# First-kind feed-forward taken on x times the norm weight, with the inverse root multiplied in afterwards

## The chip, the cores and the metric

The kernel runs on one core of one Trainium2 chip. The metric is the device time of one execution in microseconds (us). The core's engines are TensorE (PE in the profile, with its weight loads as PEld), VectorE (DVE), ScalarE (ACT), GpSimd (POOL) and SyncE (SP, which here only issues DMAs). Each engine works through its own instructions in the order in which they were written, and waits on semaphores for the others.

## What is computed

Two transformer blocks of a first kind run one after the other, then two of a second kind, on 512 tokens of width 1024 in float32. The change touches the first kind alone. One of its layers, cut to what matters here:

```python
m = hybrid_mixer(rms_norm(x, norm_mix_pre), ...)      # ends in a product with w_out
x = x + rms_norm(m, norm_mix_post)                    # norm N2
h = rms_norm(x, norm_ffn_pre)                         # norm N3
g, u = jnp.split(h @ w_gate_up, 2, axis=-1)           # 1024 -> 2 x 2816
f = (jax.nn.silu(g) * u) @ w_down
x = x + rms_norm(f, norm_ffn_post)                    # norm N4

def rms_norm(x, g): return x * lax.rsqrt(jnp.mean(x * x, -1) + eps) * g
```

Beside this the second kind needs a "modulation" for each of its layers, silu(c) @ w_mod: one vector of 48 x 128 numbers from a weight of 48 parts of 512 KB each. The first-kind layers compute it on DVE while TensorE works on the feed-forward.

## The kernel before

The state x lies transposed in SBUF as xT, 8 channel tiles (KT = 8) of 128 channels by 512 tokens. Every product is made in three passes: both operands are split into a high part and a rest (hHi and hLo for activations, wHi and wLo for weights), and each tile of 128 output channels takes 8 x 3 = 24 matmuls of 128x512 (`gemm`, L464), wHi with hi, wLo with hi, wHi with lo.

**Weights.** A weight tile is a chunk of 512 KB. SP loads chunk c into slot c % 4 of `wring` (RING = 4, `load_chunk`, L403); ACT copies it to wHi slot c % 2 (CUTS = 2, `cut_high`, L418); POOL subtracts to get wLo (`cut_rest`, L440) and adds to the semaphore w_cut. SP may load chunk c when chunk c - 4 has been cut. ACT cuts chunk c + 2 when the tile of chunk c is finished (`follow`). The first-kind chunks by number: 72 to 79 the output product of the mixer (WO), 80 to 123 gate and up tiles alternating (GU, 22 of each, FT = 22), 124 to 147 the down product (DN, three chunks for each of 8 tiles).

**Results.** Tiles of a product go to two PSUM banks psG in turn. A tile can start when the one two before it has been read out of its bank.

**Between WO and GU.** DVE squares and adds the WO tiles while they come (`branch`, L1488, L1489, L359). Then PE sums over channels (L535), ACT takes the root (L574), DVE inverts (L579), and PE spreads the inverse over partitions (L569): norm N2. DVE scales the 8 tiles (L1496); POOL adds five of them to xT (L1262) and DVE three, those of BY_DVE = (2, 5, 7), which it keeps in PSUM (`kept`), so that its add L1499 has one operand in PSUM. ACT squares each tile of xT (L526), PE sums them, and root, inverse and spread follow once more: norm N3. DVE multiplies xT by weight and inverse root (`normed`, L1293), ACT copies the high part (L481), POOL and DVE subtract to get hLo (L489, L1290), and PE starts the first GU tile. `keep_awake` issues small matmuls on the identity (L547) in the waits.

**In the feed-forward loop** (11 rounds of two gate/up pairs) ACT takes silu out of the gate's bank (L1240), DVE multiplies with the up tile's bank (L1522) and splits the result into hidHi and hidLo (L1525, L1526), then does two modulation parts (`modulate`, L1510, L1511). SP loads modulation part n into slot n % 2 of `modw`, between the weight chunks: `mod_weights`, called by `next_chunks` after each chunk, waits until part n - 2 is used, and loads part n (L773). So the parts stand in SP's queue at fixed places among the chunks: part m behind chunk 82 + m. Parts 46 and 47 come in a loop of their own (L777 to L783), each behind two more DN chunks. DVE does parts 44 to 47 after the loop and before it starts to read the DN tiles:

```python
L1532  for n in range(2 * FT, MODS):
           modulate(n)
       ...
       branch(g_DN, t_N4, 11, V1_FFNPOST, 1, branch_2)
```

Of the kernel before, what the change touches and what calls it, by code (L numbers as in the profile page):

```python
# [24 lines left out]
F32R = mybir.dt.float32r  # L25
# [217 lines left out]
def program(nc, t, out):  # L243
    ctx = ExitStack()
    with ctx:
# [34 lines left out]
        hid_full = sem("hid_full")  # L280
        mod_in, mod_used = sems("mod_in", 2), sem("mod_used")
# [133 lines left out]
        def cut_high(act, c, i=None, Kc=0):  # L415

            until(act, w_full[c % RING], 16 * (c // RING + 1) if i is None else i * (16 * Kc // RING) + 16 * (c // RING + 1))
            act.activation(wHi[:, c % CUTS, :, :], wring[:, c % RING, :, :], ACT.Copy).then_inc(w_high, 1)  # L418
# [18 lines left out]
        def cut_rest(pool, c, i=None):  # L437

            until(pool, w_high, c + 1 if i is None else i * RING + (c + 1))
            pool.tensor_tensor(wLo[:, c % CUTS, :, :], wring[:, c % RING, :, :], wHi[:, c % CUTS, :, :], ALU.subtract).then_inc(w_cut[c % CUTS], 1)  # L440
# [10 lines left out]
        def gemm(pe, u, c, rhs, kts, i=None, Ku=0, Kc=0, start=True, stop=True, ready=None, used=True):  # L451
# [7 lines left out]
            hi, lo = rhs  # L459
            for j, k in enumerate(kts):  # L460
                for n, (w, r) in enumerate(((wHi, hi), (wLo, hi), (wHi, lo))):
                    if ready is not None and n != 1:
                        pe.wait_ge(*ready(j)[n // 2])
                    mm = pe.matmul(psG[:, G.slot(u), :], w[:, c % CUTS, k, :], r(j),  # L464
                                   start=start and j == 0 and n == 0, stop=stop and j == len(kts) - 1 and n == 2)
            if used:
                mm.then_inc(G.filled(u) if stop else w_used, 1)

# [147 lines left out]
        mask = at("mask", 23552, DL, DL_KEYS)  # L616
        branch_1 = at("branch_1", 0, KT, SEQ)
# [34 lines left out]
        g_DN = g_GU + 2 * FT  # L652
# [100 lines left out]
        for l in range(DEPTH):  # L753
            with nc.Block() as block:
# [3 lines left out]
                def _(sp):  # L758
# [5 lines left out]
                    next_chunks(sp, w, l, RING, (CH1_GU - RING) // RING + 1)  # L764
# [22 lines left out]
                    sp.wait_ge(tmp_full, 4 * KT)  # L787
# [6 lines left out]
                def _(pe):  # L794
# [187 lines left out]
                    keep_awake(pe, 11)  # L982
# [3 lines left out]
                    keep_awake(pe, 5)  # L986


                    with pe.Fori(0, FT // 2) as i:
                        for j in range(4):  # L990
                            gemm(pe, g_GU + j, CH1_GU + j, h, all_k, i, 4, 4, ready=None if j else h_done(1))
# [13 lines left out]
                    norm_pe_quarters(pe, t_X, KT, KT, 1)  # L1005
# [3 lines left out]
                def _(act):  # L1009
# [215 lines left out]

                    for j in range(KT):
                        follow(act, CH1_WO + j, g_WO + j)
                    act.preload_act_table(ACT.Sqrt)
                    norm_act_quarters(act, t_N2)
                    norm_act_squares(act, st, t_N3, lambda j: xT[:, j, :], KT, lambda j: act.wait_ge(*shared(x_full, xd_full)(j)))  # L1230
                    norm_act_quarters(act, t_N3)
                    act.preload_act_table(ACT.Silu)
                    high_act(act, 2 * KT, kept(whole), tiles(hHi), KT, tmp_full, h_high)
                    act.wait_ge(cb_in, 16)
                    act.activation(cb[:, :], cb[:, :], ACT.Silu).then_inc(cb_full, 1)
                    with act.Fori(0, FT // 2) as i:
                        for j in range(2):
                            act.wait_ge(hid_full, i * 2 + j + 1)
                            act.wait_ge(*G.is_full(g_GU + 2 * j, i, 4))
                            act.activation(sl[:, j, :], psG[:, G.slot(g_GU + 2 * j), :], ACT.Silu).then_inc(G.emptied(g_GU + 2 * j), 1)  # L1240
                            for k in (2 * j, 2 * j + 1):
                                follow(act, CH1_GU + k, g_GU + k, i, 4, 4)
# [8 lines left out]
                    norm_act_squares(act, st, t_X, tiles(xT), KT, lambda j: act.wait_ge(*shared(x_full, xd_full, 1)(j)))  # L1251
# [4 lines left out]
                def _(pool):  # L1256
                    def add_branch(buf, n0):
                        for j in range(KT):
                            if j in BY_DVE:
# [8 lines left out]
                    cut_rests(pool, CH1_AB + CUTS, CH1_GU + CUTS)  # L1268
                    add_branch(branch_1, KT)
                    rest_pool(pool, KT, tiles(whole), tiles(hHi), tiles(hLo), KT, h_high, h_full)  # L1270
                    cut_rests(pool, CH1_GU + CUTS, CH1)
                    next_rest(pool, (0, 1))
                    add_branch(branch_2, 3 * KT)
# [3 lines left out]
                def _(dve):  # L1277
# [201 lines left out]
                    def branch(g0, tt, r, gain, n, buf):  # L1479
# [13 lines left out]
                        rstd = norm_dve_quarters(dve, tt, r, 2 * n + 1)  # L1493
                        for j in range(KT):
                            b = kept(buf)(j)
                            dve.scalar_tensor_tensor(b, buf[:, j, :], vec[:, gain + j:gain + j + 1], rstd, ALU.mult, ALU.mult).then_inc(tmp_full, 1)  # L1496
                            if j in BY_DVE:
                                dve.wait_ge(tmp_full, KT * (2 * n + 1) + j + 1)
# [4 lines left out]
                    branch(g_WO, t_N2, 9, V1_MIXPOST, 0, branch_1)  # L1503
                    dve.wait_ge(tmp_full, 2 * KT)
                    normed(t_N3, 10, V1_FFNPRE, 1)
# [7 lines left out]

                    dve.wait_ge(cb_full, 1)
                    with dve.Fori(0, FT // 2) as i:
                        did.enter(i, 7)
                        for j in range(2):
                            g, u = g_GU + 2 * j, g_GU + 2 * j + 1
                            until(dve, *G.is_read(g, i, 4))
                            until(dve, *G.is_full(u, i, 4))  # L1520
                            hid = psS[:, 0, 512 * j:512 * j + 512]
                            dve.tensor_tensor(hid, sl[:, j, :], psG[:, G.slot(u), :], ALU.mult).then_inc(G.emptied(u), 1)  # L1522
                            until(dve, *G.is_read(u, i, 4))
                            k = i * 2 + j
                            did(dve.tensor_copy(hidHi[:, k, :], hid))  # L1525
                            dve.tensor_tensor(hidLo[:, k, :], hid, hidHi[:, k, :], ALU.subtract).then_inc(hid_full, 1)  # L1526
                            modulate(2 * j, i)
                            modulate(2 * j + 1, i)
                        until(dve, mod_used, i * 4 + 4)
                        did(dve.tensor_copy(mod1[:, bass.ds(i * 4, 4)], small[:, 9:13]))  # L1530
                        did.leave(FT // 2)
# [1032 lines left out]
```

## Time and profile before

| | before |
|---|---|
| median of 3 runs | 3233.81 us (3233.41 to 3235.51) |
| span of the profiled execution, first to last instruction | 3232.1 us |
| PE busy | 3169.8 us, 98% |
| PE weight loads busy | 2537.2 us, 78% |
| DVE, ACT, POOL busy | 43%, 42%, 42% |

The span is 1.7 us below the median. The profile comes from one execution; a busy PE is not PE at its peak, because matmuls overlap in the records: each 128x512 matmul is shown with some 0.39 us, and starts 0.227 us after the one before it. So PE's share says little, and the distances between starts say much. The first kind runs twice (two layers), and its layers repeat each other to within about 0.1 us around the place of the change: the last WO matmul of layer 0 starts at 581.83 us, and that of layer 1 at 1542.99 us.

### The profile page before, as it was taken

Reading aid. Unit: us, or ns where it says so; the run is one execution under the profiler, and the core shown is the slowest. Engines: PE = TensorE matmul, PEld = TensorE weight load, DVE = VectorE, ACT = ScalarE, POOL = GpSimd, SP = SyncE. Lnnn points to the kernel's source line nnn. Section 1 sums busy time; section 2 is a strip of 40 time slices with the busy share of each in tenths; the row PEclk is TensorE's granted clock in tenths of the full one; section 3 lists DMA queues with packets and bytes.
Section 4 is the critical chain, followed back from the end, with each engine's and each line's share of the span. In section 5 each row is a group of like instructions: output and inputs, shape, how many; then the busy total and the mean of one; then the engine's idle time right before and its main releaser. Section 6 shows DMA issues by size and latency. Waiting matters only on the chain. (4 is left out here: it accounts for less than half of the span.)

```text
span 3232.1 us, 45316 instructions
## 1 busy us (share of the span) xinstructions
PE 3169.8 (98%) x15912; PEld 2537.2 (78%) x15912; DVE 1388.0 (43%) x2604; ACT 1347.7 (42%) x2111; POOL 1349.9 (42%) x685
## 2 busy tenths in 40 slices
PE   9999999999999999999999999999999999999999
PEld 7778888788887778888788876777888867778887
DVE  5743335555416733335555424953112148531211
ACT  6765554322227765563322224453222245532222
POOL 3233333444443233334444443544444534444444
PEclk9999999999999999999999999999999999999999
DMA  3222222355522122222355523212323232122232
GB/s 142 65 75 89 88 88 79 118 187 196 183 95 87 60 87 79 84 88 91 121 198 183 181 87 113 73 34 80 96 96 104 96 114 66 40 78 97 97 102 87
DMA packets 93595, 333.28 MB, mean 103 GB/s; under 512 B 10864, under 2 KB 12080, under 8 KB 93232
## 3 DMA queue, kind: packets, MB, share of 16 engines
q1 hardware_dynamic: 91760, 325.52, 29.6%
q10 hardware_dynamic: 1728, 6.36, 0.5%
q8 instruction: 64, 1.05, 0.1%
q14 instruction: 43, 0.35, 0.0%
HBM read 329.69 MB, written 8.44 MB: 105 GB/s over the span
## 5 line engine op out<-in xcount | busy, mean ns | idle before, releaser
L440 POOL TENSOR_TENSOR wLo<-wring,wHi 128x1024 fp32r<-128x1024 f32 x482 | 1163.3, 2414 | 1703.1 <-ACT wHi L418 1702.9
L464 PE MATMUL psG<-hHi,wHi 128*128 128x512 f32 x2992 | 1183.4, 396 | 5.8 <-ACT whole L1913 2.0
L464 PE MATMUL psG<-hLo,wHi 128*128 128x512 f32 x2992 | 1169.9, 391 | 9.7 <-POOL hLo L489 8.7
L464 PE MATMUL psG<-hHi,wLo 128*128 128x512 f32 x2992 | 1165.4, 390 | 0.0
L418 ACT ACTIVATE wHi<-wring 128x1024 fp32r<-128x1024 f32 x482 | 510.1, 1058 | 959.9 <-PE psG L464 952.7
L464 PEld LDWEIGHTS psG<-hHi,wHi 128*128 128x128 f32 x2992 | 562.1, 188 | 143.4 <-issue 29.1
L464 PEld LDWEIGHTS psG<-hLo,wHi 128*128 128x128 f32 x2992 | 561.5, 188 | 141.3 <-POOL hLo L489 24.0
L464 PEld LDWEIGHTS psG<-hHi,wLo 128*128 128x128 f32 x2992 | 562.6, 188 | 113.4 <-issue 0.5
L464 PE MATMUL psG<-hidLo,wHi 128*128 128x512 f32 x704 | 273.9, 389 | 0.0
L464 PE MATMUL psG<-hidHi,wHi 128*128 128x512 f32 x704 | 273.9, 389 | 0.0
L464 PE MATMUL psG<-hidHi,wLo 128*128 128x512 f32 x704 | 273.9, 389 | 0.0
L2369 DVE TENSOR_TENSOR psS<-tmp,psG 128x512 f32<-128x512 f32 x44 | 30.6, 696 | 371.0 <-PE psG L464 371.0
L1511 DVE CUSTOM_DVE_ANT_0 modw<-modw,cb 128x1024 f32<-128x1024 f32 x96 | 163.8, 1707 | 4.7
L1023 ACT ACTIVATE tmp<-psG 32x512 f32<-32x512 f32 x256 | 151.2, 591 | 24.3 <-PE psG L464 20.8
L464 PEld LDWEIGHTS psG<-hidHi,wHi 128*128 128x128 f32 x704 | 132.2, 188 | 28.0
L464 PEld LDWEIGHTS psG<-hidLo,wHi 128*128 128x128 f32 x704 | 132.2, 188 | 27.5
L464 PEld LDWEIGHTS psG<-hidHi,wLo 128*128 128x128 f32 x704 | 132.2, 188 | 27.0
L1433 DVE CUSTOM_DVE_ANT_0 soft<-psS,mask 128x768 f32<-128x768 f32 x64 | 61.0, 953 | 154.6 <-issue 154.6
L1522 DVE TENSOR_TENSOR psS<-tmp,psG 128x512 f32<-128x512 f32 x44 | 30.6, 696 | 216.9 <-PE psG L464 216.9
L1318 DVE SCALAR_TENSOR_TENSOR ra<-psG,ropec 128x512 f32<-128x512 f32 x44 | 30.4, 691 | 215.4 <-ACT tmp L1023 215.4
L1488 DVE COPY branch<-psG 128x512 f32 x32 | 22.1, 692 | 193.1 <-PE psG L464 192.0
L2067 ACT ACTIVATE tmp<-psG 128x512 f32<-128x512 f32 x44 | 26.3, 599 | 186.9 <-PE psG L464 186.9
(332 smaller groups left out, 3265.0 us busy)
## 6 DMA issues: line engine op xcount, KB each, us to landing
wring<-in_w SPq DMA_DIRECT2D x490, 512.0 KB, 3.3
modw<-in_wmod SPq DMA_DIRECT2D x96, 512.0 KB, 5.5
e_copies<-e_rows ACTq DMA_DIRECT2D x8, 512.0 KB
T_tab<-e_copies SPq DMA_DIRECT2D x4, 1024.0 KB, 5.6
mask<-in_mask SPq DMA_DIRECT2D x2, 1536.0 KB, 6.0
xin_sb<-in_x SPq DMA_DIRECT2D x4, 512.0 KB, 5.3
e_copies<-e_rows ACTq DMA_DIRECT2D x8, 256.0 KB
out<-o_sb SPq DMA_DIRECT2D x4, 512.0 KB, 3.4
```

The source lines that it names most:

```text
L418: act.activation(wHi[:, c % CUTS, :, :], wring[:, c % RING, :, :], ACT.Copy).then_inc(w_high, 1)
L440: pool.tensor_tensor(wLo[:, c % CUTS, :, :], wring[:, c % RING, :, :], wHi[:, c % CUTS, :, :], ALU.subtract).then_inc(w_cut[c % CUTS], 1)
L464: mm = pe.matmul(psG[:, G.slot(u), :], w[:, c % CUTS, k, :], r(j), start=start and j == 0 and n == 0, stop=stop and j == len(kts) - 1 and ...
L1023: ins = act.activation(rot[32 * a:32 * a + 32, slot, :], ps[32 * b:32 * b + 32, :], ACT.Copy, scale=QSCALE[slot])
L1318: dve.scalar_tensor_tensor(ra[:, :], ps, QSCALE[slot], ropec[:, :], ALU.mult, ALU.mult).then_inc(emptied[0], 1)
L1433: dve.tensor_tensor_reduce(Sm[:, s, :], psS[:, S.slot(u), 0:DL_KEYS], mask[:, n // 2, :], 1.0, -3.0e38, ALU.add, ALU.max, stat[:, s, 0:1]) ...
L1488: did(dve.tensor_copy(buf[:, i * 4 + j, :], ps))
L1511: dve.tensor_tensor_reduce(modw[:, j % 2, :], modw[:, j % 2, :], cb[:, :], 1.0, 0.0, ALU.mult, ALU.add, small[:, 9 + j % 4:10 + j % 4]).th ...
L1522: dve.tensor_tensor(hid, sl[:, j, :], psG[:, G.slot(u), :], ALU.mult).then_inc(G.emptied(u), 1)
L2067: act.activation(tmp[:, j, :], psG[:, G.slot(g_GU2 + 2 * j), :], ACT.Silu).then_inc(G.emptied(g_GU2 + 2 * j), 1)
L2369: dve.tensor_tensor(hid, tmp[:, j, :], psG[:, G.slot(u), :], ALU.mult).then_inc(G.emptied(u), 1)
```

## The change

Norm N3 is taken out of the way of the first products. With w the norm's weight and r the inverse root of a token, (x * w * r) @ W = ((x * w) @ W) * r, so the products run on x * w.

- ACT copies xT times weight straight to hHi and squares xT into `whole`; DVE makes hLo from xT, weight and hHi (`rest_x`, one `scalar_tensor_tensor` whose two tensors are both in SBUF), in between the scalings of `branch`. POOL adds all 8 tiles to xT.
- The squares are first added on POOL (three adds) and DVE (two), and PE sums three partial tiles.
- The first two GU tiles go channel tile by channel tile (`gemm_pair`) into two other PSUM banks. The weights of the first four GU tiles are cut early, into buffers of their own (`first_cuts`).
- DVE multiplies each gate and each up tile by r (r3) out of its bank; silu runs in SBUF; the product with the up tile follows.
- `modulate` moves: in the loop one part stands between the gate's and the up's multiplication, one after the split. Parts 0 and 1 run ahead of the first tiles, 2 and 3 with the first pairs. The loop has 10 rounds, and SP's `mod_weights` goes with the chunks from 88 on where it went with those from 84 on.

The diff, cut to its core:

```diff
@@ SP
-                    next_chunks(sp, w, l, RING, (CH1_GU - RING) // RING + 1)
+                    next_chunks(sp, w, l, RING, CH1_WO // RING)
...
-                    next_chunks(sp, w, l, CH1_GU + RING, 2 * FT // RING, mod_weights)
+                    next_chunks(sp, w, l, CH1_WO + RING, 2)
+                    for c in range(CH1_GU + RING, CH1_GU + 2 * RING):
+                        sp.wait_ge(w_cut[c % CUTS], (c - RING) // CUTS + 1)
+                        load_chunk(sp, w, l, c)
+                    next_chunks(sp, w, l, CH1_GU + 2 * RING, 2 * FT // RING - 1, mod_weights)
                     c = CH1_DN + RING
-                    for n in range(2 * FT + 2, MODS):
-                        for _ in range(2):
+                    for n in range(2 * FT - 2, MODS):
+                        for _ in range(2 if n >= 2 * FT else 0):
                             sp.wait_ge(w_cut[c % CUTS], (c - RING) // CUTS + 1)
                             load_chunk(sp, w, l, c)
                             c += 1
@@ PE
+        def gemm_pair(pe, c, outs, cuts, rhs, ready, done):
...
+            for j in range(KT):
+                high, rest = ready(j)
+                pe.wait_ge(*high)
+                for out, (wh, wl) in zip(outs, cuts):
+                    pe.matmul(out, wh[:, j, :], hi(j), start=j == 0, stop=False)
+                    pe.matmul(out, wl[:, j, :], hi(j), start=False, stop=False)
+                pe.wait_ge(*rest)
+                for out, (wh, wl) in zip(outs, cuts):
+                    mm = pe.matmul(out, wh[:, j, :], lo(j), start=False, stop=j == KT - 1)
...
-                    norm_pe_quarters(pe, t_N3, 0, KT, 1)
-                    keep_awake(pe, 5)
+                    gemm_pair(pe, CH1_GU, first_banks, first_cuts[0:2], h, both(counted(h_high, KT), counted(hd_full, len(BY_DVE))), first_full)
...
+                    third(0, 3)
+                    pe.wait_ge(xs_pool, 3)
+                    pe.wait_ge(xs_dve, 2)
+                    pe.wait_ge(xs_act, KT)
+                    pe.wait_ge(*T.is_free(t_N3))
+                    quarter_sums(pe, t_N3, (whole[:, 0, :], whole[:, 4, :], whole[:, KT - 1, :])).then_inc(T.filled(t_N3), 1)
+                    third(3, 7)
                     norm_pe_spread(pe, t_N3, 2)
+                    third(7, KT)
+                    gemm(pe, g_GU + 1, CH1_GU + 3, h, all_k, cut=first_cuts[3])
@@ ACT
                     for j in range(KT):
-                        follow(act, CH1_WO + j, g_WO + j)
...
+                        act.wait_ge(x_full, j + 1)
+                        act.activation(hHi[:, j, :], xT[:, j, :], ACT.Copy, scale=vec[:, V1_FFNPRE + j:V1_FFNPRE + j + 1]).then_inc(h_high, 1)
+                        act.activation(whole[:, j, :], xT[:, j, :], ACT.Square).then_inc(xs_act, 1)
...
+                            follow(act, CH1_GU + 4 + 2 * j, g_GU + 2 + 2 * j, i, 4, 4)
+                            silu(j, 3 + j, i)
+                            follow(act, CH1_GU + 5 + 2 * j, g_GU + 3 + 2 * j, i, 4, 4)
@@ DVE
+                    def rest_x(j):
+                        dve.wait_ge(h_high, KT + j + 1)
+                        dve.scalar_tensor_tensor(hLo[:, j, :], xT[:, j, :], vec[:, V1_FFNPRE + j:V1_FFNPRE + j + 1], hHi[:, j, :],
+                                                 ALU.mult, ALU.subtract).then_inc(hd_full, 1)
...
+                    with dve.Fori(0, FT // 2 - 1) as i:
+                        did.enter(i, 9)
                         for j in range(2):
+                            g, u = g_GU + 2 + 2 * j, g_GU + 3 + 2 * j
+                            until(dve, *G.is_full(g, i, 4))
+                            dve.tensor_tensor(sl[:, j, :], psG[:, G.slot(g), :], r3[:, :], ALU.mult).then_inc(G.emptied(g), 1)
                             until(dve, *G.is_read(g, i, 4))
+                            dve.sem_inc(gate_full, 1)
+                            modulate(4 + 2 * j, i)
                             until(dve, *G.is_full(u, i, 4))
+                            dve.tensor_tensor(psS[:, 0, 512 * j:512 * j + 512], psG[:, G.slot(u), :], r3[:, :], ALU.mult).then_inc(G.emptied(u), 1)
                             until(dve, *G.is_read(u, i, 4))
+                            hidden(j, i * 2 + (2 + j), 3 + j, i)
+                            modulate(5 + 2 * j, i)
```

## Rows read from the trace of the kernel before

**Rows 1.** The page, busy time (share of the span) and instructions of each engine

```profile
PE 3169.8 (98%) x15912; PEld 2537.2 (78%) x15912; DVE 1388.0 (43%) x2604; ACT 1347.7 (42%) x2111; POOL 1349.9 (42%) x685
```

**Rows 2.** Stages: stretch, length, busy us of each engine, granted clock, DMA share, GB/s

```profile
580.00:604.00 24.00, 20.75 (x190) 15.75 (x189) 15.49 (x23) 12.22 (x18) 12.30 (x10) 1.00 0.16 65
604.00:842.00 238.00, 237.82 (x1050) 196.66 (x1049) 119.95 (x203) 59.10 (x69) 105.98 (x46) 1.00 0.51 183
```

**Rows 3.** Timeline of PE (start, duration, what): last WO matmul, GU tile starts, DN start

```profile
581.83 0.40 PE L464 MATMUL psG<-hLo,wHi 128*128 128x512 f32 x1
...
600.78 0.47 PE L464 MATMUL psG<-hHi,wHi 128*128 128x512 f32 x1 [0.48 <-ACT hHi L481]
...
608.21 0.39 PE L464 MATMUL psG<-hHi,wHi 128*128 128x512 f32 x1
...
842.12 0.39 PE L464 MATMUL psG<-hidHi,wHi 128*128 128x512 f32 x1
```

**Rows 4.** Timelines of DVE, POOL and ACT: the additions to x and the squares

```profile
587.28 1.41 DVE L1496 SCALAR_TENSOR_TENSOR branch<-branch,vec,psT 128x512 f32<-128x512 f32 x2 [1.25 <-PE psT L569]
...
588.10 2.51 POOL L1262 TENSOR_TENSOR xT<-xT,branch 128x512 f32<-128x512 f32 x2 [2.36 <-DVE branch L1496]
...
589.41 0.63 ACT L526 ACTIVATE sq<-xT 128x512 f32<-128x512 f32 x1 [4.38 <-POOL xT L1262]
```

**Rows 5.** Line and timelines: DVE operations on two SBUF tensors, alone and beside POOL

```profile
L1368 DVE SCALAR_TENSOR_TENSOR soft<-soft,stat x32: 750/751/754, 50.4 to 1124.4; 128x512 f32<-128x512 f32 x32
...
1989.08 3.02 DVE L2217 SCALAR_TENSOR_TENSOR score<-relu,iws,score 128x256 f32<-128x256 f32 x2 [2.85 <-ACT relu L1966]
...
1988.85 2.38 POOL L440 TENSOR_TENSOR wLo<-wring,wHi 128x1024 fp32r<-128x1024 f32 x1 [5.43 <-ACT wHi L418]
...
854.36 3.45 DVE L1511 CUSTOM_DVE_ANT_0 modw<-modw,cb 128x1024 f32<-128x1024 f32 x1
...
854.34 2.40 POOL L440 TENSOR_TENSOR wLo<-wring,wHi 128x1024 fp32r<-128x1024 f32 x1 [3.04 <-ACT wHi L418]
```

**Rows 6.** Timelines of ACT, POOL and DVE in one pair of the loop

```profile
820.56 1.06 ACT L418 ACTIVATE wHi<-wring 128x1024 fp32r<-128x1024 f32 x1 [3.89 <-PE psG L464]
826.00 0.60 ACT L1240 ACTIVATE tmp<-psG 128x512 f32<-128x512 f32 x1 [4.38 <-PE psG L464]
826.50 1.05 ACT L418 ACTIVATE wHi<-wring 128x1024 fp32r<-128x1024 f32 x1
...
821.70 2.40 POOL L440 TENSOR_TENSOR wLo<-wring,wHi 128x1024 fp32r<-128x1024 f32 x1 [2.56 <-ACT wHi L418]
...
820.63 0.69 DVE L1522 TENSOR_TENSOR psS<-tmp,psG 128x512 f32<-128x512 f32 x1 [5.03 <-PE psG L464]
...
825.25 1.23 DVE L1511 CUSTOM_DVE_ANT_0 modw<-modw,cb 128x1024 f32<-128x1024 f32 x1
```

**Rows 7.** DMA issues (KB each, median us to landing), and landings of modw in the loop

```profile
wring<-in_w SPq DMA_DIRECT2D x490, 512.0 KB, 3.3
modw<-in_wmod SPq DMA_DIRECT2D x96, 512.0 KB, 5.5
...
DMA to landing us min/median/max: 3.4/5.5/6.1
...
modw<-in_wmod SPq DMA_DIRECT2D x1, 512.0 KB, 4.6
```

**Rows 8.** Timelines of DVE, POOL and SP: last modulation part, first DN tiles

```profile
862.47 0.06 DVE L1510 MEMSET tick<- 128x1 f32 x1 [3.08 <-DMA modw<-in_wmod]
...
864.03 2.29 DVE L1536 TENSOR_TENSOR modv<-mod,bmod 128x48 f32<-128x48 f32 x1
...
869.52 0.70 DVE L1489 TENSOR_TENSOR psS<-branch,psG 128x512 f32<-128x512 f32 x1
...
873.38 2.40 POOL L440 TENSOR_TENSOR wLo<-wring,wHi 128x1024 fp32r<-128x1024 f32 x1 [1.68 <-ACT wHi L418]
...
857.85 0.33 SPq L783 DMA_DIRECT2D modw<-in_wmod x1
```

**Rows 9.** Stage after the DN tiles, as in Rows 2

```profile
962.00:985.00 23.00, 18.14 (x168) 13.69 (x168) 15.10 (x22) 11.86 (x18) 11.55 (x9) 0.93 0.24 83
```

More of the change, by code:

```diff
@@ L449, in cut_rests, with gemm @@
                 cut_rest(pool, c)
-        def gemm(pe, u, c, rhs, kts, i=None, Ku=0, Kc=0, start=True, stop=True, ready=None, used=True):
+        def gemm(pe, u, c, rhs, kts, i=None, Ku=0, Kc=0, start=True, stop=True, ready=None, used=True, cut=None):
             pe.wait_ge(w_cut[c % CUTS], c // CUTS + 1 if i is None else i * (Kc // CUTS) + (c // CUTS + 1))
@@ L651, in program @@
         g_GU = g_WO + KT
[L652 removed]
+        g_DN = g_GU + 2 * FT - 2
         def in_DL(j, i):
@@ L981, in _, with third @@
                     norm_pe_spread(pe, t_N2, 1)
-                    keep_awake(pe, 11)
-                    norm_pe_quarters(pe, t_N3, 0, KT, 1)
-                    keep_awake(pe, 5)
+                    keep_awake(pe, 10)
+                    gemm_pair(pe, CH1_GU, first_banks, first_cuts[0:2], h, both(counted(h_high, KT), counted(hd_full, len(BY_DVE))), first_full)
+                    def third(k0, k1):
+                        gemm(pe, g_GU, CH1_GU + 2, (tiles(hHi, k0), tiles(hLo, k0)), range(k0, k1), start=k0 == 0, stop=k1 == KT,
+                             used=k1 == KT, cut=first_cuts[2])
+                    third(0, 3)
[5 more added lines that the diff above has]
+                    third(3, 7)
                     norm_pe_spread(pe, t_N3, 2)
-                    keep_awake(pe, 5)
-                    with pe.Fori(0, FT // 2) as i:
+                    third(7, KT)
+                    gemm(pe, g_GU + 1, CH1_GU + 3, h, all_k, cut=first_cuts[3])
+                    with pe.Fori(0, FT // 2 - 1) as i:
                         for j in range(4):
-                            gemm(pe, g_GU + j, CH1_GU + j, h, all_k, i, 4, 4, ready=None if j else h_done(1))
+                            gemm(pe, g_GU + 2 + j, CH1_GU + 4 + j, h, all_k, i, 4, 4)
                     with pe.Fori(0, 2) as i:
@@ L1231, in _ @@
                     norm_act_quarters(act, t_N3)
                     act.preload_act_table(ACT.Silu)
[L1233 to L1236, printed above, removed]
-                        for j in range(2):
[L1238 to L1242, printed above, removed]
+                    act.wait_ge(rstd_full, 3)
@@ L1267, in _ @@
                     cut_rests(pool, CUTS, CH1_AB + CUTS)
-                    cut_rests(pool, CH1_AB + CUTS, CH1_GU + CUTS)
+                    cut_rests(pool, CH1_AB + CUTS, CH1_GU)
+                    for n in range(4):
+                        cut_rest(pool, CH1_GU + n, out=first_cuts[n])
                     add_branch(branch_1, KT)
-                    rest_pool(pool, KT, tiles(whole), tiles(hHi), tiles(hLo), KT, h_high, h_full)
-                    cut_rests(pool, CH1_GU + CUTS, CH1)
+                    for j in range(1, 4):
+                        pool.wait_ge(xs_act, j + 1)
+                        if j > 1:
+                            pool.wait_ge(xs_pool, j - 1)
+                        pool.tensor_tensor(whole[:, 0, :], whole[:, 0, :], whole[:, j, :], ALU.add).then_inc(xs_pool, 1)
+                    cut_rests(pool, CH1_GU + 4, CH1)
                     next_rest(pool, (0, 1))
-                    add_branch(branch_2, 3 * KT)
+                    add_branch(branch_2, 2 * KT, BY_DVE)
                 @block.vector
```

129 lines of the change are left out of this document (97 added, 32 removed).

## The prediction, made before the changed kernel ran

> **What bounds the kernel now.** I began with the busy times: PE 98%, every other engine at 43% or less [rows 1]. So the end is set by PE's queue, and the question is where PE waits or does filler. Two stages show it: from 580 to 604 us PE is called busy for 20.75 us, but with 190 instructions, most of them the identity filler, while from 604 to 842 nothing but real matmuls run [rows 2]. The timeline of PE gives the price. WO's last matmul starts at 581.83, GU's first at 600.78, its second tile at 608.21, and DN at 842.12 [rows 3]. From 608.21 to 842.12 lie 43 tiles of 24 matmuls, so a tile takes 5.44 us. Tile 0 takes 7.43, so in effect GU starts at 602.77, 20.7 us after WO. Two layers hold 41 us of this, the most that could be had here. In steady state DVE, ACT and POOL all wait for PE [rows 6], with some slack, and that slack is what the change spends.
>
> **Part 1, the front of GU.** What goes is the wait for norm N3: squares, sum, root, table load, inverse, spread, rescale. New order: POOL's additions to x set the pace. The first starts at 588.10 and two take 2.51 us [rows 4], so 1.26 each; x tile 0 is ready at 589.4, ACT's hHi (priced as the 0.63 of the square [rows 4]) at 590.1. There `gemm_pair` starts: 6 matmuls for each channel tile, 1.36 us, 10.9 for 8. Undisturbed it ends at 600.9 to 601, where two tiles of before end at 613.65.
>
> But `rest_x` reads two SBUF tensors on DVE while POOL adds without a pause. The trace has two kinds of row for such an operation. 32 of one line take 0.75 us each, those that I followed with POOL idle [rows 5]. The one at 1989.08 meets a POOL subtraction of 1988.85 to 1991.23: two short ones together take 3.02 us, and the modulation part of 854.36 takes 3.45 beside POOL's 2.40, against 1.23 alone [rows 5, 6]. I take the second kind: they exclude each other for whole instructions. Then each channel tile costs 1.26 + 0.70 = 1.96 us: x tile 1 at 590.6, x tile 7 at 590.6 + 6 x 1.96 = 602.4, hHi 7 at 603.1, hLo 7 behind one more POOL operation at 605.0, the pair done at 605.5. Next 9 matmuls (2.0); the partial squares (three POOL and two DVE additions, again in turns) come at 609.0, the sums take 1.0 (610.0), 12 matmuls 2.7, spread 1.0, 3 matmuls 0.7 and one tile 5.44: tile 3 ends at 619.8. Before it ended at 608.21 + 3 x 5.44 = 624.5. **Gain 4.7 us a layer**; bounds 10.2 (no exclusion: pair at 600.9, the sum then right behind it) and 2 (worse turns).
>
> The Trainium skill, "SBUF — State Buffer", section "Who interferes with whom", says that a VectorE instruction with two SBUF inputs and a GpSimd instruction that reads SBUF exclude each other for the whole instruction, and that the order of issue decides who blocks. The 0.75 us row alone would give a gain of 10.2, this rule 4.7 at best; the rows at 1989.08 and 854.36 agree with it.
>
> The early weights are free. They add four cuts to ACT (1.06) and POOL (2.40, [rows 6]) between 572 and 584.5, where both would wait for the WO tiles, and the POOL additions start at 588.1. The moved silu of cb and its table loads stand behind WO tile 0, with 5.44 us to the next tile.
>
> **Part 2, the loop's own work.** DVE gains one operation of 0.69 for the gate and one for the up tile in place of none (five of 0.69 and two parts of 1.23 to 2.2: at most 8 of 10.88 us for a pair). That alone fits.
>
> **Part 3, where the modulation parts now stand in SP's queue.** This decides. The diff moves `mod_weights` from chunk 84 to chunk 88, so part m is issued behind chunk 86 + m, not 82 + m. Chunk 86 + m waits for the cut of chunk 82 + m, which is GU tile m + 2, and ACT cuts that one when tile m is full. But DVE wants part m right behind tile m (m even, ahead of the up tile's multiplication). So the load can't be early; before, the lead was four tiles more. The path, F being the time at which tile m is full: cut 0.2 + 1.06, 0.08 to POOL, 2.40: F + 3.74 [rows 6]. To SP's issue 0.19, the part's DMA 0.47 behind the chunk's. Landing: a lone chunk takes 3.3 us, the parts in the loop 3.4 to 6.1, median 5.5 with four transfers together, and 4.6 for the one behind a single chunk [rows 7]; here there is one chunk ahead, and I take 4.4. DVE starts part m at F + 8.9 and frees the up bank at about F + 11.2 where PE wants it at F + 10.88.
>
> The odd part closes a ring that is longer: gate multiplied 0.70, to ACT 0.12, silu 0.50 (start to start), cut 1.06 + 0.08, POOL 2.40, SP 0.19 + 0.47, landing 4.4, wake 0.1, part m + 1 1.35, to the next gate 0.1: 11.47 us, and 0.18 on average for the copy of four results behind every second pair. 11.65 for a pair against PE's 10.88: 0.77 lost in each of 19 pairs, **14.6 us a layer**. Bounds: with a landing of 3.4 the odd ring just fits, but the even path and the exclusion with POOL still leave some 10; with 5.5 to 5.6 it is 0.77 + 1.1 for each, some 32. I lean to 14.6, as 4.6 is the nearest row.
>
> **Part 4, the last parts.** Parts 42 and 43 now lie in the tail loop, and 44 to 47 each stand behind two DN chunks. So part 47 waits for chunk 135, that for the cut of chunk 131, that for DN tile 1 to be full. In the present trace POOL ends that cut at 873.38 + 2.40 = 875.78 [rows 8]; now part 47 is issued at 857.85 [rows 8]. After the change: 875.78 + 0.19 + 0.47 + 4.4 = 880.8, and DVE does 47 only then. From its memset (862.47) to the first DN bank's release (869.52 + 0.70) there are 7.75 us now [rows 8], of which 2.1 are the 2.29 us operation on 48 numbers, caught beside POOL; POOL will be idle, so 5.7: bank 0 is free at 886.7. DN tile 2 wants it at 842.12 + 2 x 14.96 = 872.0. **PE stands still for 14.6 us a layer** (times relative to DN's start). Bounds 13.5 (landing 3.4) to 17 (with the 2.1 back). The only cover today is 1.8 us. After such a stop the granted clock matters: in the stage 962 to 985, with a stop of 2.9 us in it, it is 0.93 of 2.4 GHz on average, so 1.6 us lost to the 1.2 GHz level [rows 9]. I take 2 us for a longer stop, bounds 0 and 4.
>
> **Sum.** A layer: -4.7 + 14.6 + 14.6 + 2.0 = +26.5. Two layers: +53. The span of 3232.1 becomes 3285.1; the median lies 1.7 above the profiled span, so 3286.8, say **3287 us**, 1.6% slower. Its own range, from the bounds of landing and clock: 3270 to 3312.
>
> **Rivals.**
> - *No exclusion for `rest_x`* (the 0.75 us rows hold beside POOL too): 5.5 us less a layer, 3276. Against it stands 1989.08.
> - *Only the tail stalls*: the landings are short or the ring has slack that I don't see, so part 3 costs nothing: -4.7 + 14.6 + 2 = 11.9 a layer, 3258. For it: 3.4 us landings exist [rows 7].
> - *Long landings in the loop*: the loop's own median of 5.5 holds though fewer transfers lie together; +17 a layer, 3321.
> - *Faster.* The stalls stay off PE. The mechanism is the place of part 47 in SP's queue: it must land by 872.0 - 5.7 = 866.3, 14.5 us ahead of what I have, which needs it to be issued by about 862, that is ahead of chunk 132 and not behind 135; and the landings in the loop must stay under about 3.6. Then Part 1 alone is left: with the exclusion 3224, without it 3213. The written order speaks against it; a gain appears from the point at which the two stalls cost less than 4.7 us together.
>
> **Chances.** Forecast 0.62; no exclusion 0.10; only the tail 0.08; long landings 0.10; faster 0.05; the rest (stalls that cancel the gain within 0.2%, or something unseen) 0.05. The range 3256 to 3312 takes in the forecast, the first two rivals and a part of the third. A measurement of this kernel can't tell less than about 0.2% (6.5 us) from no change. Faster 0.05, same 0.03, slower 0.92.
>
> **What the changed profile would show.** GU's first matmul near 590 and the pair done near 605.5 with `rest_x` at 1.5 to 2 us (or near 601 with 0.75); in the loop DVE's modulation memset waiting for the modw DMA in each pair, and a gate-to-gate distance of 11.6 in place of 10.88; ahead of DN tile 2 one PE wait of some 15 us, released by DVE's first copy of a DN tile, with DVE waiting for part 47; a lower clock just behind it. If DVE's waits for modw are absent from the loop, Part 3 is wrong; if PE goes from DN tile 1 to tile 2 without a gap, Part 4 is.

## The result: 1.6% slower, and the profile after

| | before | after |
|---|---|---|
| median, us | 3233.61 (3232.67 to 3235.51, 4 runs) | 3284.31 (3281.95 to 3286.14, 4 runs) |
| ratio | 1 | 1.0155, 95% interval 1.0142 to 1.0167 |
| profiled execution, us | span 3232.1 | 3284.89, span 3283.1 |
| mean granted clock, of 2.4 GHz | 0.997 | 0.992 |

The forecast was 3287 us, in a range of 3256 to 3312. The page of after has, for busy time and instructions (before: [rows 1]):

```profile
PE 3180.6 (97%) x15764; PEld 2526.8 (77%) x15764; DVE 1451.1 (44%) x2684; ACT 1353.3 (41%) x2115; POOL 1359.8 (41%) x687
```

PE has 148 instructions fewer and yet 10.8 us more of busy time. A low clock is a part of that: the matmuls from 893.04 us on are shown with 0.63 to 0.80 us in place of 0.39; the rest I did not take apart. The timeline of PE gives the stages, as [rows 3] did: WO's last matmul, the first of `gemm_pair`, GU tile 4, DN's first, and the first one behind a stop.

```profile
580.67 0.40 PE L468 MATMUL psG<-hLo,wHi 128*128 128x512 f32 x1
...
589.12 0.47 PE L482 MATMUL psS<-hHi,fcHi 128*128 128x512 f32 x1 [0.80 <-ACT hHi L1281]
...
616.91 0.39 PE L468 MATMUL psG<-hHi,wHi 128*128 128x512 f32 x1
...
849.21 0.39 PE L468 MATMUL psG<-hidHi,wHi 128*128 128x512 f32 x1
...
893.04 0.80 PE L468 MATMUL psG<-hidHi,wHi 128*128 128x512 f32 x1 [13.76 <-DVEq L1561]
```

I cut every kernel into the same three stretches. *Front*: from WO's last matmul to the first of GU tile 4. For before that is 608.21 + 3 x 5.44 - 581.83 = 42.70 us, for after 616.91 - 580.67 = 36.24. *Loop*: tile 4 to DN's first matmul, 40 tiles or 217.6 us without a loss; after has 232.30. *DN*: from its first matmul to the third from its end (528 in all), 119.0 us before. Against before, in us, for the two layers (two numbers where they differ):

| kernel | front | loop | DN | median, us |
|---|---|---|---|---|
| after | -6.5 | +14.7, +17.7 | +15.5, +16.2 | 3284.31 |
| e1_loads_early | -6.5, -6.6 | 0 | 0, +0.3 | 3221.65 |
| e2_tail_only | -6.5, -6.6 | +16.8, +16.2 | 0 | 3253.68 |
| e3_loop_only | -6.5, -6.6 | 0 | +15.7, +16.4 | 3252.47 |
| e5_before_shifted | 0 | 0 | +16.5, +15.9 | 3272.40 |
| e6_parts_behind_split | -6.5, -6.6 | +14.1, +14.4 | +16.4, +16.9 | 3280.48 |
| e7_silu_behind_cut | -6.5, -6.6 | +13.3, +13.5 | +16.0, +16.8 | 3280.21 |
| e8_no_pair | -2.1 | 0 | +0.2, 0 | 3229.18 |
| e4_rest_psum | -9.7 | 0 | 0 | 3215.47 |
| e9_half_parts | -6.5, -6.6 | +15.6 | +15.3 | 3282.95 |
| e10_parts_psum | -6.5, -6.6 | +12.1, +11.5 | +16.4, +16.7 | 3276.26 |
| e11_silu_psum | -6.5, -6.6 | +9.6, +9.1 | +16.3, +16.1 | 3274.47 |
| e12_all_three | -6.5, -6.6 | +2.2, +4.0 | +15.1, +15.9 | 3256.24 |

For after, -6.5 + 14.7 + 15.5 = +23.7 in the first layer and -6.5 + 17.7 + 16.2 = +27.4 in the second: +51.1, and the spans differ by 51.0. The stretches outside differ by up to some 2 us each from kernel to kernel.

In the loop DVE now waits for its transfers, 37 times and 75.2 us in the first layer's (before: not once there; its eight waits for modw, 15.7 us, all stand behind the loops), and PE waits for DVE. The waits of after, whole span (engine, line, what it waited for: us, times, longest):

```profile
DVE tick L1598 <- DMA modw<-in_wmod: 207.3, 83, 9.1
...
PE psG L468 <- DVEq L1561: 27.7, 2, 13.9
...
PE psG L468 <- DVE tmp L1635: 11.4, 19, 1.2
...
PE psG L468 <- DVE psS L1640: 4.8, 23, 0.7
```

L1635 frees the gate's bank and L1640 the up tile's, so PE waits for both. The two waits add up to less than the loss, because the matmul records overlap: from start to start, the steps at the starts of the tiles hold 14.0 of the 14.7 us of the first layer's loop.

One pair of it, from the timelines of DVE, ACT, POOL and SP (before: [rows 6]):

```profile
708.38 0.68 DVE L1635 TENSOR_TENSOR tmp<-psG,rms 128x512 f32<-128x512 f32 x1
...
709.15 0.63 ACT L1291 ACTIVATE tmp<-tmp 128x512 f32<-128x512 f32 x1 [4.26 <-DVEq L1637]
709.69 1.04 ACT L420 ACTIVATE wHi<-wring 128x1024 fp32r<-128x1024 f32 x1
...
710.81 2.39 POOL L443 TENSOR_TENSOR wLo<-wring,wHi 128x1024 fp32r<-128x1024 f32 x1 [3.44 <-ACT wHi L420]
...
713.91 0.33 SPq L799 DMA_DIRECT2D modw<-in_wmod  x1
...
718.00 0.06 DVE L1598 MEMSET tick<- 128x1 f32 x1 [0.43 <-DMA modw<-in_wmod]
718.10 1.69 DVE L1599 CUSTOM_DVE_ANT_0 modw<-modw,cb 128x1024 f32<-128x1024 f32 x1
...
720.52 0.69 DVE L1635 TENSOR_TENSOR tmp<-psG,rms 128x512 f32<-128x512 f32 x1 [0.41 <-DVE mod L1645]
```

Read from top to bottom this is the ring: gate multiplied, silu, cut, rest, issue, landing (718.00 - 713.91 = 4.09), part, and the next gate 12.14 us after the one before it, where PE offers one each 10.88. Pairs without the copy of results (L1645) are shorter; on average it is (217.6 + 14.7) / 20 = 11.6.

### The profile page after: what moved, and what is told of

It is laid out like the page before. It is cut to its first block and busy times, and to the rows that moved or that the text cites. A ratio compares the mean times of both kernels' runs of the same rounds, so it can differ in the third digit from the quotient of the medians.

```text
span 3283.1 us, 45034 instructions
## 1 busy us (share of the span) xinstructions
PE 3180.6 (97%) x15764; PEld 2526.8 (77%) x15764; DVE 1451.1 (44%) x2684; ACT 1353.3 (41%) x2115; POOL 1359.8 (41%) x687
## 5 line engine op out<-in xcount | busy, mean ns | idle before, releaser
L443 POOL TENSOR_TENSOR wLo<-wring,wHi 128x1024 fp32r<-128x1024 f32 x474 | 1144.9, 2416 | 1753.4 <-ACT wHi L420 1753.2
L468 PE MATMUL psG<-hHi,wHi 128*128 128x512 f32 x2928 | 1164.7, 398 | 22.1 <-DVE tmp L1635 11.4
L468 PE MATMUL psG<-hLo,wHi 128*128 128x512 f32 x2928 | 1145.9, 391 | 6.6 <-POOL hLo L510 5.7
L468 PE MATMUL psG<-hHi,wLo 128*128 128x512 f32 x2928 | 1141.7, 390 | 0.0
L420 ACT ACTIVATE wHi<-wring 128x1024 fp32r<-128x1024 f32 x474 | 501.0, 1057 | 983.0 <-PE psG L468 975.8
L468 PEld LDWEIGHTS psG<-hHi,wHi 128*128 128x128 f32 x2928 | 550.5, 188 | 178.2 <-issue 48.2
L468 PEld LDWEIGHTS psG<-hLo,wHi 128*128 128x128 f32 x2928 | 550.2, 188 | 133.1 <-POOL hLo L510 16.5
L468 PEld LDWEIGHTS psG<-hHi,wLo 128*128 128x128 f32 x2928 | 551.2, 188 | 109.7 <-issue 0.5
L2484 DVE TENSOR_TENSOR psS<-tmp,psG 128x512 f32<-128x512 f32 x44 | 30.6, 696 | 371.0 <-PE psG L468 371.0
L1599 DVE CUSTOM_DVE_ANT_0 modw<-modw,cb 128x1024 f32<-128x1024 f32 x96 | 165.2, 1721 | 4.8
L1291 ACT ACTIVATE tmp<-tmp 128x512 f32<-128x512 f32 x44 | 27.8, 631 | 185.1 <-DVEq L1637 180.7
```

What stands on the lines that cost most here:

```text
L420: act.activation(wHi[:, c % CUTS, :, :] if out is None else out[0], wring[:, c % RING, :, :], ACT.Copy).then_inc(w_high, 1)
L443: pool.tensor_tensor(lo, wring[:, c % RING, :, :], hi, ALU.subtract).then_inc(w_cut[c % CUTS], 1)
L468: mm = pe.matmul(psG[:, G.slot(u), :], w[:, k, :], r(j), start=start and j == 0 and n == 0, stop=stop and j == len(kts) - 1 and n == 2)
L1291: act.activation(sl[:, j, :], sl[:, j, :], ACT.Silu).then_inc(silu_full, 1)
L1599: dve.tensor_tensor_reduce(modw[:, j % 2, :], modw[:, j % 2, :], cb[:, :], 1.0, 0.0, ALU.mult, ALU.add, small[:, 9 + j % 4:10 + j % 4]).th ...
L2484: dve.tensor_tensor(hid, tmp[:, j, :], psG[:, G.slot(u), :], ALU.mult).then_inc(G.emptied(u), 1)
```

## The experiments

Theory Q, the prediction's: the front gains, and the places of the modulation parts in SP's queue cost it twice, in the loop (part m behind chunk 86 + m) and ahead of DN tile 2 (part 47 behind chunk 135). Rivals: the new work on DVE and ACT slows the loop whatever the loads do; the tail is the only loss; the front's gain comes from the moved inverse root and not from the pair.

**e1_loads_early.** The changed kernel with SP's order alone undone: part m behind chunk 83 + m in the loop, one chunk for each of the last parts. That is one chunk later than in the kernel before (82 + m).

```
                    plain_chunk(CH1_GU + 4)
                    plain_chunk(CH1_GU + 5)
                    with sp.Fori(0, 2 * FT // RING - 1) as i:
                        for j in range(RING):
                            mod_weights(i, j)
                            ... chunk CH1_GU + 6 + j + 4 * i
                    c = CH1_DN + 2
                    for n in range(2 * FT - 2, MODS):
                        plain_part(n)
                        plain_chunk(c)
                        c += 1
```

> The changed kernel with only SP's queue reordered: modulation part m is issued behind weight chunk 83 + m (changed kernel: 86 + m), also in the tail, where part 47 stands behind chunk 130 and not behind 135. Theory Q (the place of the parts in SP's queue costs both the 14.7 and 17.7 us in the loops and the 15.5 and 16.2 us in the DN stages): all of that goes, what is left is the front's gain of 6.5 us a layer against the kernel before, so about 3284.3 - 64 = 3220 us, and DVE's waits for modw are gone from the loop. Rival D (DVE's added multiplications and the part between gate and up are too much by themselves): the loop's 32 us stay and only the DN stage is cured, about 3253 us.

3221.65 us (3219.55 to 3222.87, 5 runs), ratio 0.9960, interval 0.9946 to 0.9974: faster than both kernels. Loop and DN are back to 217.60 and 119.0 with all the new work in place, so the whole loss hangs on where SP issues the parts. In the loop of e1 DVE no longer waits for a landing; its two longest waits from 617 to 842 us are for PE:

```profile
DVE psS L1650 <- PE psG L468: 62.7, 20, 3.1
DVE tmp L1645 <- PE psG L468: 12.9, 20, 0.8
```

**e2_tail_only** and **e3_loop_only** take the two places apart. e2 is the changed kernel with its last four parts at their places of before (44 and 45 behind no further chunk, 46 and 47 behind 129 and 131); e3 has e1's loop and the changed kernel's last parts.

```
-                        for _ in range(2 if n >= 2 * FT else 0):
+                        for _ in range(2 if n >= 2 * FT + 2 else 0):
```

> The changed kernel with only the tail of the modulation loads put back to the order of the kernel before (parts 44 and 45 behind no further DN chunk, part 46 behind chunk 129, part 47 behind chunk 131). Theory Q: PE's wait ahead of DN tile 2 (13.9 us in layer 0) and the low clock behind it go, 31.7 us for two layers, about 3253 us; the loop still loses 32 us. If the wait ahead of DN tile 2 came from something else (the banks, the cut of DN's weights), the time stays at 3284.

> The changed kernel with the parts of the loop issued early (part m behind chunk 83 + m) and the tail left as it is (part 47 behind chunk 135). Theory Q: the loop's loss of 14.7 + 17.7 us goes and the DN stage keeps its wait of 14 us a layer, about 3252 us. Rival D (DVE's work itself): no change in the loop, 3284 us.

3253.68 us (ratio 1.0060, interval 1.0043 to 1.0077) and 3252.47 us (1.0055, 1.0038 to 1.0072). Above e1 that is 32.0 and 30.8, together 62.8; after is 62.7 above e1. The two losses are separate and add up.

**e5_before_shifted.** The kernel before, with nothing but the changed kernel's order in SP's queue.

```
-                    next_chunks(sp, w, l, CH1_GU + RING, 2 * FT // RING, mod_weights)
+                    for c in range(CH1_GU + RING, CH1_GU + 2 * RING):
+                        ...
+                    next_chunks(sp, w, l, CH1_GU + 2 * RING, 2 * FT // RING - 1, mod_weights)
...
-                    for n in range(2 * FT + 2, MODS):
-                        for _ in range(2):
+                    for n in range(2 * FT - 2, MODS):
+                        for _ in range(2 if n >= 2 * FT else 0):
```

> The kernel before with one part of the change alone: SP's parts one ring later (part m behind chunk 86 + m, the tail as in the changed kernel, part 47 behind chunk 135); DVE, ACT, POOL and PE untouched, both parts of a pair still behind the split. Theory Q with the ring (gate multiplied - silu - cut - load - part - next gate): the ring does not exist here, since silu takes the gate out of the bank on ACT; a part lands 8.9 us after its tile is full, DVE wants the even one at 7.9 and the odd one lands at 14.3, done by 15.7, ahead of the next up tile at 16.3, so the loop costs nothing; the DN stage stops PE for about 14 us a layer: 3233.6 + 31 = 3265 us. Rival S (late parts alone make the loop's loss, whatever DVE's order): 3265 + 30 = 3295 us.

3272.40 us (ratio 1.0118, interval 1.0101 to 1.0135); the profiled execution took 3266.36, and the other three 3272.2 to 3273.2. Where those 6 us lie no trace shows, so it stays open. DN loses as in after, but the loop loses nothing, although DVE waits for its landings longer than in after (92.0 us against 75.2 in the first layer's loop; waits of e5, whole span):

```profile
DVE tick L1513 <- DMA modw<-in_wmod: 238.7, 88, 8.9
...
PE psG L464 <- DVEq L1494: 27.7, 2, 13.9
```

So a late part alone doesn't hold the loop; it does so in the new loop body. What differs there, as I read it, is that DVE frees the gate's bank too: in before that was ACT's silu [rows 6], and a late part kept only the up tile's bank from PE. No run changes that alone, in before or after.

**e4_rest_psum** and **e8_no_pair** are e1 with one thing more, for the front. In e4 `rest_x` subtracts a PSUM tile in place of hHi, so that the low half of the feed-forward's input is wrong (left out). In e8 `gemm_pair` multiplies its two tiles one after the other.

```
-                        dve.scalar_tensor_tensor(hLo[:, j, :], ..., hHi[:, j, :],
+                        dve.scalar_tensor_tensor(hLo[:, j, :], ..., psT[:, T.slot(t_N2), :],
...
-            for j in range(KT):
-                ...
-                for out, (wh, wl) in zip(outs, cuts):
+            for out, (wh, wl) in zip(outs, cuts):
+                for j in range(KT):
```

> The kernel of e1_loads_early, in which rest_x subtracts a PSUM tile in place of hHi, so that only one of its tensors is in SBUF. This leaves out the true rest hLo of the feed-forward's input: a run for time alone. Theory P (DVE's two-SBUF-tensor operation and POOL's additions exclude each other): rest_x takes 0.75 us in place of 1.12 to 1.46, POOL's eight additions 10.2 us in place of 12.7, the pair's channel tiles come at PE's own 1.36 us, the partial sums are ready about 3 us sooner: GU tile 4 starts at 33.2 us behind WO's last matmul in place of 36.2, two layers 6 us, about 3216 us. Rival: POOL's pace is its own or ACT's (two operations a tile); then nothing changes, 3221.7 us.

> The kernel of e1_loads_early, with the first two GU tiles one after the other in place of channel tile by channel tile. Tile 0 follows the channel tiles and ends where the pair ended; tile 1 then takes 5.44 us of its own, less 0.7 us that PE waited for the partial sums: GU tile 4 starts 4.5 to 4.7 us later, at 40.8 us behind WO's last matmul, 9 us for two layers, about 3231 us. So of the front's gain of 6.5 us a layer the pair holds 4.7 and the moved inverse root by itself 1.8. Rival: the pair gains nothing because PE waits for the channel tiles anyway; then 3222 us.

3215.47 us (0.9941, 0.9928 to 0.9955) and 3229.18 us (0.9985, 0.9976 to 0.9994). Of the front's 6.5 us a layer the pair holds 4.4 and the rest of the new order, the moved inverse root above all, 2.1; the exclusion costs 3.2 that could be had beside them. Timelines of DVE and POOL in after, then in e4:

```profile
592.29 1.12 DVE L1584 SCALAR_TENSOR_TENSOR hLo<-xT,vec,hHi 128x512 fp32r<-128x512 f32 x1
...
586.95 12.71 POOL L1326 TENSOR_TENSOR xT<-xT,branch 128x512 f32<-128x512 f32 x8 [3.77 <-DVE branch L1567]
```

```profile
591.59 0.74 DVE L1594 SCALAR_TENSOR_TENSOR hLo<-xT,vec,psT 128x512 fp32r<-128x512 f32 x1
...
586.89 10.12 POOL L1336 TENSOR_TENSOR xT<-xT,branch 128x512 f32<-128x512 f32 x8 [3.80 <-DVE branch L1577]
```

With two SBUF operands `rest_x` takes 1.12 and POOL's additions 12.71 / 8 = 1.59 each; with one it is 0.74 and 1.27.

**e6_parts_behind_split** and **e7_silu_behind_cut** try two links of the loop's ring, each in the changed kernel. e6 puts the even part behind the split of the hidden tile, where the odd one is; e7 puts silu behind ACT's second cut.

```
-                            modulate(4 + 2 * j, i)
...
+                            modulate(4 + 2 * j, i)
                             modulate(5 + 2 * j, i)
```

```
-                            silu(j, 3 + j, i)
                             follow(act, CH1_GU + 5 + 2 * j, g_GU + 3 + 2 * j, i, 4, 4)
+                            silu(j, 3 + j, i)
```

> The changed kernel with both modulation parts of a pair behind the split, as in the kernel before; SP's queue is left as changed. Theory R (the ring: gate multiplied on DVE, silu, cut, load, odd part, next gate): the odd part still stands ahead of the next gate's multiplication, so the ring of 11.5 to 11.8 us against 10.88 stays and the loops lose 12 to 17 us each: about 3284 us. Rival B (what costs is the even part ahead of the up tile, which holds the up bank): the loops' 32 us go, 3252 us.

> The changed kernel with one line of ACT's loop moved: silu of the gate behind the second cut of the pair and not ahead of it. Theory R: that opens the ring, since the cut for the odd part's load no longer waits for the gate's multiplication. Left is the even part ahead of the up tile (bank free 0.3 us late, about 3 us a layer). The loops lose 3 to 6 us each in place of 14.7 and 17.7: about 3260 us. Rival B (the even part): silu's place changes nothing, 3284 us or more.

3280.48 us (1.0144, 1.0128 to 1.0159) and 3280.21 us (1.0152, 1.0137 to 1.0168). The even part's place by itself isn't the cause. The second missed my figure: I had taken silu for the link that closes the ring and expected 3 to 6 us a layer to be left; 13.4 were. In e7's trace both parts still stand in front of a multiplication that frees a bank, and both are stretched beside POOL's cut (timelines of POOL and DVE in e7):

```profile
704.95 2.39 POOL L443 TENSOR_TENSOR wLo<-wring,wHi 128x1024 fp32r<-128x1024 f32 x1 [3.90 <-ACT wHi L420]
...
706.29 2.13 DVE L1599 CUSTOM_DVE_ANT_0 modw<-modw,cb 128x1024 f32<-128x1024 f32 x1
...
708.36 0.68 DVE L1635 TENSOR_TENSOR tmp<-psG,rms 128x512 f32<-128x512 f32 x1
```

**e9 to e12** therefore take three things apart in the changed kernel: the landing, the stretch, and silu's place. In e9 and e12 only the left half of 46 of 48 modulation parts is loaded (256 KB), and the product of the loop's parts goes to PSUM and not back to `modw`; in e10, e11 and e12 the loop's parts read silu(c) from PSUM.

```
-    sp.dma_start(modw[:, n % 2, :], t["wmod"][l, n])
+    sp.dma_start(modw[:, n % 2, 0:DM // 2], t["wmod"][l, n][:, 0:DM // 2])
```

```
+                    cbP = psS[:, 1, :]
+                    did(dve.tensor_copy(cbP, cb[:, :]))
...
-    dve.tensor_tensor_reduce(modw[:, j % 2, :], modw[:, j % 2, :], cb[:, :], ...
+    dve.tensor_tensor_reduce(modw[:, j % 2, :], cbP, modw[:, j % 2, :], ...
```

> The changed kernel with only the left half (256 KB in place of 512 KB) of each modulation part from 2 on loaded, so 46 of the 48 modulation parts are wrong; nothing else is shorter: DVE still multiplies over 1024 columns (in the loop its product goes to a spare PSUM bank). Theory T: what closes the loop's ring is the landing of a late part. Then a landing shorter by about 1 us takes the ring from 11.6 below PE's 10.88 us a pair, GU tile 4 to DN falls from 232 to 235 us to under 221, the stop ahead of DN tile 2 falls by the same 1 us to about 13, and the time is about 3254 us. Rival X: the ring goes through DVE and the order of issue alone, and the landing has slack: no more than the stop's 1 us a layer is won, 3281 us.

> The changed kernel with silu(c) copied once a layer into a spare PSUM bank (1024 columns), and the loop's 40 modulation parts reading it from there: one SBUF operand in place of two. Everything is computed. Theory T: in the loop the parts stretch to 1.6 to 2.75 us only because two SBUF operands and POOL's cut exclude each other, and each ring runs through one such part. Then parts take about 1.2 us, a pair 11.2 in place of 11.6, the loop loses about 7 us a layer in place of 15 to 18, and the time is about 3266 us. Rival N: the stretch is slack, the ring is landing and silu alone: 3284 us.

> Both edits together: silu behind ACT's second cut, and the loop's parts with one operand in PSUM. Theory T: the late parts hold PE through two rings, one through silu and one through the release of the gate's and the up tile's bank behind a stretched part; silu's place alone won 1.4 to 4.2 us a layer because the second stayed. With both gone a pair takes 10.88 to 10.95, the loop loses 0 to 2 us a layer, and the time is about 3256 us. Rival N: the landing alone sets it, 3280 us as with silu's place alone.

3282.95 us (1.0149, 1.0132 to 1.0165), 3276.26 us (1.0127, 1.0110 to 1.0144) and 3274.47 us (1.0121, 1.0104 to 1.0138). All three missed Theory T's figure. In e9 the landing fell by only 0.6 us (transfers of the loop, after and e9):

```profile
DMA to landing us min/median/max: 3.9/4.1/5.0
```

```profile
DMA to landing us min/median/max: 3.2/3.5/5.2
```

and it bought nothing in the loop: where the part now starts just ahead of POOL's cut it is the cut, a link of the same ring, that is stretched. In e9's two loops 16 of the 78 cuts take over 2.6 us, in after 1 (DVE and POOL in e9):

```profile
700.83 1.23 DVE L1599 CUSTOM_DVE_ANT_0 psS<-modw,cb 128x1024 f32<-128x1024 f32 x1
...
700.94 3.37 POOL L443 TENSOR_TENSOR wLo<-wring,wHi 128x1024 fp32r<-128x1024 f32 x1 [4.31 <-ACT wHi L420]
```

A stretched cut costs only where a late part stands behind it: in e1, with the parts issued early, 20 of the 39 cuts of each loop take 3.3 us, and the loop loses nothing.

In e10 the stretch is gone (all 80 parts of the two loops, min/median/max in ns):

```profile
L1599 DVE CUSTOM_DVE_ANT_0 modw<-psS,modw x80: 1224/1225/1227, 633.8 to 1835.0; 128x1024 f32<-128x1024 f32 x80
```

which wins 2.6 and 6.2 us a layer. e11 wins another 2.5 by silu's place and still loses 9.1 to 9.6, 0.47 for each of 20 pairs. I followed one of its even parts (ACT, POOL, SP, DVE and PE in e11):

```profile
703.47 1.06 ACT L420 ACTIVATE wHi<-wring 128x1024 fp32r<-128x1024 f32 x1 [4.45 <-PE psG L468]
...
704.61 2.39 POOL L443 TENSOR_TENSOR wLo<-wring,wHi 128x1024 fp32r<-128x1024 f32 x1 [3.64 <-ACT wHi L420]
...
707.94 0.33 SPq L799 DMA_DIRECT2D modw<-in_wmod  x1
...
712.42 0.06 DVE L1598 MEMSET tick<- 128x1 f32 x1 [4.08 <-DMA modw<-in_wmod]
712.53 1.23 DVE L1599 CUSTOM_DVE_ANT_0 modw<-psS,modw 128x1024 f32<-128x1024 f32 x1
...
713.68 0.70 DVE L1642 TENSOR_TENSOR psS<-psG,rms 128x512 f32<-128x512 f32 x1
...
714.52 0.47 PE L468 MATMUL psG<-hHi,wHi 128*128 128x512 f32 x1 [0.29 <-DVE psS L1642]
```

The tile behind the full one starts at 703.19, which I take as F; then come cut, rest to 707.00, issue, landing, part to 713.76, and the up tile is multiplied by 714.4. That is 11.2 behind F, and PE starts in this bank 11.3 behind F, where it wants it at 10.88. It is the path that Part 3 of the prediction names first. e12 shortens its landing with both other links gone; its parts take 1.23 us like e11's.

> Silu behind the second cut, silu(c) read from PSUM in the loop's parts, and the half transfers of 256 KB as well (46 of 48 modulation parts are wrong; DVE's work is the same, its product goes to PSUM in the loop). With silu and the stretch gone the loop still lost 9.1 to 9.6 us a layer, 0.49 for a pair, with landings of 4.1 to 4.5. Theory T: that rest is the plain late path, cut, POOL, SP, landing, part, up tile's multiplication: 11.2 against 10.88. A landing shorter by 0.6 takes it below 10.88: the loop loses 0 to 3 us a layer, the stop ahead of DN tile 2 stays, shorter by 0.6: about 3258 us. Rival N: the rest has another cause than the landing: 3273 us.

3256.24 us (1.0069, 1.0053 to 1.0086), as Theory T had it. The loop loses 2.2 and 4.0 us; the stop ahead of DN tile 2 is 13.4 in place of 13.9 (PE's waits in e12):

```profile
PE psG L468 <- DVEq L1561: 26.6, 2, 13.4
```

## Why the prediction was right

- *Bound, and what there was to gain.* Right: PE sets the end in all kernels, and the front could be shortened.
- *Part 1, -4.7 a layer.* Measured -6.5, between the bounds of 2 and 10.2. The exclusion is there: without it e4 has -9.7, close to the upper bound (10.2 as written; its own terms add up to 10.7). What was mis-sized is the price of the exclusion: 5.5 us a layer expected, 3.2 measured. I charged 0.70 for each channel tile (1.26 + 0.70 = 1.96); the first matmuls of the channel tiles, at 590.63, 592.33 and 594.03, are 1.70 apart, so it was 0.44. As I read it, DVE's 1.12 us row holds a part of its own wait, and its work overlaps the hand-over; no row shows where the one gives way to the other. The Trainium skill, "SBUF — State Buffer", section "Who interferes with whom", says that one blocks the other for the whole instruction; e4's 0.74 against 1.12 and 1.27 against 1.59 agree in kind. The pace of 1.70 in place of 1.26 + 0.70 does not: in this chain of short operations one tile costs less than both whole ones, and the measurement decides. The pair ended 21.9 us behind WO's last matmul, where I had 23.7.
- *Part 2, DVE's new operations fit.* Right: e1 has them all and loses nothing in the loop.
- *Part 3, +14.6.* Measured 14.7 in the first layer and 17.7 in the second. The mechanism, late parts by their place in SP's queue, is shown by e1 and e2. The size was hit by luck in part, with two errors that cancel: the landing is 4.1 and not 4.4, and the odd part beside POOL's cut takes 1.6 to 1.7 in the first layer's loop and not 1.35. The ring has more links in parallel than I wrote down. Taking silu's place away alone (e7) left 13.4; the rest is held, as e10 to e12 bear out, because the bank of the gate is freed behind the odd part, and that of the up tile behind the even one. In the order e10, e11, e12 the loop's mean loss of 16.2 falls by 4.4 (the stretch), 2.5 (silu) and 6.2 (0.6 us of landing), and 3.1 are left. These shares hold in this order only: the landing's 0.6 by itself (e9) won 0.6 of the mean and silu by itself 2.8. Why the second layer of after loses 3 us more than the first is open.
- *Part 4, +14.6 and +2.0.* Measured 13.9, twice, and +1.6 and +2.3 behind it. Part 47 is issued at 883.20 and has landed at 887.25, that is 38.0 behind DN's start where I had 38.7 (880.8 - 842.12); from its memset to the first release of a bank there are 5.7 us, as I had said. (In the recorded sum 880.8 + 5.7 was written as 886.7; it is 886.5, so the stop by its own terms was 14.5.) Timelines of SP and DVE in after:

```profile
883.20 0.43 SPq L813 DMA_DIRECT2D modw<-in_wmod  x1
...
887.25 0.06 DVE L1598 MEMSET tick<- 128x1 f32 x1 [7.39 <-DMA modw<-in_wmod]
...
892.23 0.70 DVE L1559 TENSOR_TENSOR psS<-branch,psG 128x512 f32<-128x512 f32 x1
```

- *The clock.* Behind the stop it stands at the 1.2 GHz level, and then at 2.4 GHz (stages of after, columns as in [rows 2], the third number from the end is the clock):

```profile
894.00:896.00 2.00, 2.00 (x6) 1.57 (x5) 1.81 (x3) 0.00 (x0) 0.00 (x0) 0.51 0.00 0
896.00:900.00 4.00, 4.00 (x19) 3.29 (x19) 0.19 (x1) 0.00 (x0) 0.00 (x0) 1.00 0.00 0
```

  In the 2 us row it is 0.51, in the one behind it 1.00: 1.6 us lost in one layer and 2.3 in the other, against the 2 that I took.
- *Sum.* +26.5 for a layer; measured +23.7 and +27.4. The front was too poor by 1.8 and the stop too long by 0.7; the second layer's loop was too good by 3. That the total came within 3 us of the forecast is in part luck, since these errors cancel; the two costs and their place are not.
- *Rivals.* "Only the tail stalls", "no exclusion" and "long landings" are refuted by e3 against after, by e4, and by the 4.1 us landings. "Faster" holds exactly where it was said to: once the parts are issued early, only the front is left, and e1 gives 3221.65 against the 3224 of that case.

## What to carry to other kernels

An in-order DMA queue is part of a loop's critical ring: before a small load is moved past one buffer-recycling load more, add up that buffer's release, the issue and the landing against the time of one round, and ask which bank's release stands behind its use. A late load can be harmless, as in e5's loop, while the engine that waits for it frees nothing that the bound engine needs soon; in the new loop body, in which that engine has one more bank to free, the same lateness cost 15 to 18 us a layer. When a change with a good part comes out slower, undo its moves in the queues first: SP's order alone separates 3284 from 3222 us here.

## What the hardware did that I had not expected

- The cost of the DVE and POOL exclusion moves with the order of start. A part that finds POOL at its cut takes longer, 2.75 us in place of 1.23 for the one at 700.40 in after; a cut that starts 0.11 us behind a part takes 3.37 in place of 2.39 (e9, above). The transfers that land 0.6 us sooner in e9 met 16 of 78 cuts in this other order, and the loop gained nothing to speak of. The Trainium skill, "SBUF — State Buffer", section "Who interferes with whom", says that issue order decides who blocks; both rows agree. POOL and DVE in after:

  ```profile
  699.68 2.39 POOL L443 TENSOR_TENSOR wLo<-wring,wHi 128x1024 fp32r<-128x1024 f32 x1 [4.25 <-ACT wHi L420]
  ...
  700.40 2.75 DVE L1599 CUSTOM_DVE_ANT_0 modw<-modw,cb 128x1024 f32<-128x1024 f32 x1
  ```

- With one of its two operands in PSUM, the same custom operation on 1024 columns took 1224 to 1227 ns in all 80 cases, beside POOL or not.
- Halving a transfer from 512 to 256 KB shortened its landing behind another transfer only from 4.1 to 3.5 us.
